# Two-layer MLA / neighbourhood-attention / mixture-of-experts step: where the last tile's down block is loaded, when the next layer's first projection block is loaded, and where a pass issues its row gathers

## What is computed

```python
def grouped_moe(h, w_router, router_bias, w_gate, w_up, w_down):
    scores = sigmoid(t @ w_router)                      # 16 experts in 4 groups
    # best group of 4 experts, then the 2 best experts of it, gates normalised
    act = silu(einsum('td,edf->tef', t, w_gate)) * einsum('td,edf->tef', t, w_up)
    act = act * gates[..., None]
    return einsum('tef,efd->td', act, w_down)           # D = 1024, expert width 256
# per layer
x = x + gate_f * grouped_moe(modulate(rmsnorm(x), shift_f, scale_f))
```

## Time and profile before

| | |
|---|---|
| runs | 1395.22, 1396.58, 1402.12 us |
| profiled execution | 1406.06 us; span of the trace 1404.2 us |
| busy: PE, DVE, ACT, POOL | 1283.3, 568.4, 339.7, 232.8 us |
| chain that ended last | PE 70%, DMA 14%, DVE 6%, issue 5%, ACT 4% |
| of it, the DMA of adds with static lists (`xrows<-big,info`) | 10% |
| of it, the DMA of adds with `last_tok` (`xrows<-big`) | 3% |
| mean granted TensorE clock | 0.978 |
| DMA traffic | 267.82 MB, 191 GB/s over the span |

### The profile page before, as it was taken

The page is one execution under the profiler, slowest core; times in us unless marked ns, Lnnn a source line. Parts: engine busy times, 40 slices in busy tenths (PEclk is TensorE's granted clock), DMA queues, the critical chain, the costliest instruction groups (busy, mean ns, idle before and its releaser), DMA issues.

```text
span 1404.2 us, 19127 instructions
## 1 busy us (share of the span) xinstructions
PE 1283.3 (91%) x7399; PEld 740.6 (53%) x7399; DVE 568.4 (40%) x1454; ACT 339.7 (24%) x823; POOL 232.8 (17%) x298
## 2 busy tenths in 40 slices
PE   5999899999999989998949999999998998999991
PEld 3665466666654554444424455656775446445440
DVE  5122344444535664444322000002664576444443
ACT  3121344444422310000012000003664231000102
POOL 7122300010010012123221100013221001211231
PEclk8999999999999999999979999999999999999996
DMA  9413211122464459999583363145122615999966
GB/s 388 148 39 153 87 62 62 62 105 78 179 247 164 152 193 390 381 380 395 118 249 125 121 225 120 61 173 165 50 66 95 242 62 225 391 379 380 337 171 210
DMA packets 45449, 267.82 MB, mean 191 GB/s; under 512 B 6980, under 2 KB 13460, under 8 KB 31520
## 3 DMA queue, kind: packets, MB, share of 16 engines
q1 hardware_dynamic: 22672, 192.85, 35.1%
q0 software_dynamic: 16928, 52.77, 13.8%
q10 hardware_dynamic: 5760, 20.97, 3.8%
HBM read 230.19 MB, written 34.81 MB: 189 GB/s over the span
## 4 chain that ended last, share of the span: by engine, by line
PE 70%; DMA 14%; DVE 6%; issue 5%; ACT 4%; DVEq 0%; ACTq 0%; POOLq 0%; SPq 0%
PE PS L851 12%; DMA xrows<-big,info 10%; PE PS L1217 10%; PE PS L1079 10%; PE PS L1127 9%; PE PS L723 8%; PE PS L1144 4%; PE PS L979 4%; PE PS L738 3%; DMA xrows<-big 3%; PE PS L1010 2%; PE PS L938 2%; PE PS L1020 2%; DVE big L1621 1%; ACT weights L1481 1%
## 5 line engine op out<-in xcount | busy, mean ns | idle before, releaser
L1079 PE MATMUL PS<-weights,ht 128*128 128x512 f32 x320 | 142.3, 596 | 2.3 <-DVE ht L1621 1.6
L1217 PE MATMUL PS<-ht,weights 128*128 128x128 f32 (+1 forms) x512 | 140.2, 434 | 1.5 <-PE PS L738 0.9
L723 PE MATMUL PS<-const,big 128*128 128x128 f32 (+2 forms) x611 | 90.1, 284 | 37.8 <-DVE big L2151 17.8
L851 PE MATMUL PS<-weights,ht 128*128 128x336 f32 (+1 forms) x320 | 118.2, 528 | 2.6 <-ACT ht L1399 1.6
L1127 PE MATMUL PS<-big 128*128 128x512 f32 x256 | 115.8, 606 | 4.7 <-DVE big L2068 4.7
L723 PEld LDWEIGHTS PS<-const,big 128*128 128x128 f32 (+2 forms) x611 | 74.1, 144 | 84.1 <-issue 58.2
L1217 PEld LDWEIGHTS PS<-ht,weights 128*128 128x128 f32 x512 | 77.8, 191 | 64.1 <-issue 64.1
L1079 PEld LDWEIGHTS PS<-weights,ht 128*128 128x128 f32 x320 | 59.0, 190 | 69.7 <-issue 69.7
L1530 ACT ACTIVATE big<-PS 128x256 f32<-128x256 f32 x34 | 13.1, 385 | 329.4 <-PE PS L1127 329.4
L851 PEld LDWEIGHTS PS<-weights,ht 128*128 128x128 f32 x320 | 61.0, 193 | 54.5 <-issue 41.1
L1127 PE MATMUL PS<-weights,big 128*128 128x512 f32 x192 | 84.4, 592 | 0.0
(11 more groups left out here) (247 smaller groups left out, 1815.3 us busy)
## 6 DMA issues: line engine op xcount, KB each, us to landing
weights<-in_ada SPq DMA_DIRECT2D x22, 2048.0 KB, 8.8
big<-in_gu SPq DMA_DIRECT2D x16, 2048.0 KB, 19.9
weights<-in_gu SPq DMA_DIRECT2D x12, 2048.0 KB, 21.1
rows<-in_down SPq DMA_DIRECT2D x18, 1024.0 KB, 12.4
weights<-in_down SPq DMA_DIRECT2D x16, 1024.0 KB, 16.0
ht<-in_gu SPq DMA_DIRECT2D x6, 2048.0 KB, 22.3
weights<-in_qkv SPq DMA_DIRECT2D x6, 2048.0 KB, 10.2
weights<-in_wo SPq DMA_DIRECT2D x4, 2048.0 KB, 8.6
```

The costliest lines, as they stand in the source:

```text
L723: return pe.transpose(dst, src, const[0:n, C_ID:C_ID + n])
L851: ins = pe.matmul(bank(4 + u % 2, n), lhs(k), rhs(k), start=(k == 0), stop=(k == ks - 1))
L1079: ins = pe.matmul(bank(4 + j), OT[:, k, t * P:(t + 1) * P], w[j][:, k, :], start=(k == 0), stop=(k == KD - 1))
L1217: ins = pe.matmul(bank(bb, n1 - n0), w[:, k, m * P:(m + 1) * P], hT[:, k, n0:n1], start=(k == 0), stop=(k == KD - 1))
```

## The change

In SP's queue the last tile's down block goes to `DN[0]`, behind a wait for the 13th down projection instead of the one that frees `DN[2]`, and in layer 0 the qkv block follows behind a wait for the 14th. POOL's pass issues both gathers in its head: the first before the copies (from list column 5, which is column 3 after the shift), with a wait for its landing before the copies; the second after the copies, before both adds. The two adds then follow one another. PE's last down projection reads `DN[0]`. All engines' instructions are otherwise the same, in number too but for a few waits and one fewer semaphore instruction of POOL's a pass.

```diff
@@ SP @@
-                sp.wait_ge(e_dn[l], trips * 2 + (STAT - 2))
+                sp.wait_ge(e_dn[l], STAT - 2)
                 last = sp.value_load(rtx[0:1, bass.ds(trips * 2 + (STAT - 1), 1)], min_val=0, max_val=E - 1)
-                sp.dma_start(DN[2], a["down"][l][bass.ds(last, 1)]).then_inc(e_dw[l][0], 16)
+                sp.dma_start(DN[0], a["down"][l][bass.ds(last, 1)]).then_inc(e_dw[l][0], 16)
                 if l == 0:
+                    sp.wait_ge(e_dn[l], STAT - 1)
                     static_load(1, 1)
@@ POOL @@
                 with pool.Fori(0, trips) as i:
+                    pool.wait_ge(e_tr[l], i * 2 + (STAT + 1))
+                    pool.nop().then_inc(e_gate, 1)
+                    rows_of(last_token(5), 1)
+                    pool.wait_ge(e_gi[l][1], i * 16 + 16 * 9)
+                    pool.wait_ge(e_gi[l][0], i * 16 + 16 * 8)
                     for par in range(2):
-                        pool.wait_ge(e_gi[l][par], i * 16 + 16 * 8)
                         pool.wait_ge(e_ys[l][par], i * 16 + 16 * 7)
                     pool.nop().then_inc(e_gate, 1)
                     pool.tensor_copy(moved_tok, last_tok[:, 2:15]).then_inc(e_next[l], 1)
...
                     pool.wait_ge(e_next[l], i * 2 + 2)
+                    pool.wait_ge(e_tr[l], i * 2 + (STAT + 2))
                     pool.nop().then_inc(e_gate, 1)
+                    rows_of(last_token(4), 0)
                     for j in range(2):
 
                         pool.wait_ge(e_yd[l], i * 2 + (STAT + j))
                         pool.wait_ge(e_ys[l][1 - j], i * 16 + (112, 128)[j])
                         pool.nop().then_inc(e_gate, 1)
                         add_rows(last_token(j), j)
-
-                        pool.wait_ge(e_tr[l], i * 2 + (STAT + 1 + j))
-                        pool.nop().then_inc(e_gate, 1)
-                        rows_of(last_token(3 + j), 1 - j)
@@ PE @@
-                down(2, e_dw[l][0], trips * 16 + 16, trips * 2 + STAT, None, 3)
+                down(0, e_dw[l][0], trips * 16 + 16, trips * 2 + STAT, None, 3)
```

## The result

The changed kernel takes 1405.23 us (median of 9 runs, 1400.83 to 1408.37), the kernel before 1399.68 us (9 runs, 1395.22 to 1402.25): ratio 1.0028, 95% interval 1.0017 to 1.0039. So it is some 3 us slower. The forecast was 1.0 us faster, and 1405.2 lies outside the range up to 1401.3. Of the 9.6 us between 1395.6 and 1405.2, 3.1 are the reference: the forecast stood on the median of three runs of the kernel before (1396.58), and nine give 1399.68. The other 6.6 are the change's own, 5.6 slower for 1.0 faster by these medians; in the two repeats the medians differ by only 3.0 and 1.9 us. That it stays within 0.5% held.

What follows compares the result with a forecast made beforehand. A handful of adds near each MoE stage's end were taken to set the end. Gains of 0.6 us (first stage) and 0.4 us (second) make 1396.58 - 1.0 = 1395.6 us, range 1391.5 to 1401.3.

Steps and rivals of the forecast that it cites:

- the stretched add 12: First stage: the early qkv block lies over add 12, which takes 10.5 us instead of 7.1 (bounds 7.1 and 11.6).
- Now it lands at 701.11 + 10.91 = 712.02: First stage: add 14's landing before the change, against 712.0 after it; issued 3.8 us later, it gains 3.8 us.
- once getting worse (1404.1): First stage: PE's product of tile 15 runs at the low clock throughout, 3.8 us more; part of a 0.16 chance.
- once gone by the change, as a gain of 3.1 us (1392.5): First stage: PE's wait shifts so that the product at 684 us keeps full clock; chance 0.04.
- 1.9 us of cover remain: Second stage: add 14 lands by 1371.8, add 15 waits for its y until about 1373.7, so the delay costs nothing.
- the prediction's own signs of being wrong: Add 10 or 11 over a microsecond slower, add 12 near 7, second-stage add 15 waiting for add 14, or 5 us off.
- Add 15 without a gather behind it: Both stages: add 15 takes 6.23 us for 6.80 in the first, 6.2 for 6.64 in the second, 0.4 gained there.
- The early down block: First stage: delays add 10 by 0.5 us (bounds nothing and 2.25); second stage: hidden by 2.8 us of cover.
- Clean gain: Rival, chance 0.22: add 12 isn't stretched much, y of tile 15 bounds the first stage's end; 2.5 us faster, 1394.1.
- The slower rival: Chance 0.16: the down block lands on add 10 in full and PE waits; 1400.3 us, or 1404.1 with the clock.
- The row on what 2 MB beside an add cost: Profile row used for add 12's size: 2 MB of qkv beside an add cost it 4.5 us.
- the estimate of an equal share: Add 12: engines alternate between queues, so the block costs it 1.2 us; first stage gains about 1.2 instead of 0.6.

Runs made afterwards that it cites:

- the two repeats: The changed kernel timed twice more with no edit, each beside its own runs of the kernel before: ratio 1.0019 both times.
- the early loads alone: Against the kernel before, only the last down block and the qkv block loaded early, POOL's loop as before: ratio 0.9995.
- the candidate: Against the changed kernel, both gathers of a pass moved behind add 14, loads still early: 0.9992 and 0.9994 to the kernel before.
- the double delay: Two memsets of 2.10 us on POOL ahead of add 14, gathers as before: 1.0023 with early loads, 1.0003 in the kernel before.

## Why the prediction was wrong

**The chain in the changed kernel was forecast well.** From add 12's issue, first stage, in us:

```
                         add 13   g17 landed   add 14   add 15   last add landed
forecast                  11.3       19.2        22.0     29.9      43.1
changed, first trace      11.9       19.6        22.7     29.6      42.6
changed, second trace     12.3         -         23.6     31.2      44.1
changed, third trace      11.4         -         22.3     30.2      43.4
before, first trace        7.8         -         18.7     30.4      44.2
before, second trace       6.9         -         16.5     28.1      41.5
```

The loads, the stretched add 12, the swap of 10.9 against some 6 us for add 14, gather 17's landing (5.8 for 6.0) and the copies came as said. Only gather 18 starts 0.6 us later behind the copies than taken (0.90 us for 0.3), and add 14 took 6.1, 6.8 and 7.1 us in the three traces for the 7.1 taken.

**The step that failed is what it was compared with**: "Now it lands at 701.11 + 10.91 = 712.02", and the 3.56 us for which add 14 was said to wait for its y. Both were read in one execution in which PE's product of tile 15 ran at the low clock. I had this clock before me in two rivals: once getting worse (1404.1), and once gone by the change, as a gain of 3.1 us (1392.5). In both the low clock counted as a property of the kernel before. It was one execution's: in 16 of the 17 traces the product is faster than 9.94 us, and in two of the three of the changed kernel it runs at full clock without any such gain. That it had already made y late, and so padded the cover in front of add 14, I didn't draw. In the second trace of the kernel before, y of tile 15 starts 24.9 us behind add 12's issue (705.48 - 680.58) and not 27.1, the wait in front of add 14 is 2.22 us and not 3.56, and the stage's last add lands 2.6 us sooner. Against that trace the forecast of 43.1 is a loss of 1.6 us, and the three measured stages (mean 43.4) one of 1.9. The reference is one trace; that the early loads alone (41.6 in their trace) timed at 0.9995 speaks for it.

**The second stage** fails in the same way, by a cover read off one execution, but not by the clock: there the product took 7.10 or 7.11 us in every trace. "1.9 us of cover remain" took y of tile 15 at 1372.38, 27.3 us behind add 12's issue. In the second and third trace of the changed kernel it starts 24.6 and 25.0 behind it (1369.51 and 1367.73):

```profile
1369.51 1.28 DVE L1624 TENSOR_TENSOR big<-PS,big 128x512 f32<-128x512 f32 x2
```

In the two traces of the kernel before it is 27.3 and 25.6, in the first of the changed kernel 29.5. How far the chain of adds runs ahead of PE when it reaches add 12 differs by that much from one execution to the next, and the cover with it. In the second and third trace add 14 is issued at 20.2 both times (forecast 19.6), and add 15 follows add 14 by 7.7 us where it follows by 10.5 when y releases it. From y of tile 15 to the read-back of the residual it is 16.9 and 16.7 us instead of 15.5; in the first trace it is 15.6. So the stage costs 1.4, 1.2 and 0.1 us. That add 15 would wait for add 14 there was among the prediction's own signs of being wrong; it came in two traces of three. With the first stage that makes 2.8 us, or 1.002. Between the stages nothing is lost: from the read-back of the first to y of tile 15 in the second it is 645.0, 644.9 and 644.9 us in the changed kernel, 645.6 and 644.9 in the kernel before.

**Sizes that were only off.** Add 15 without a gather behind it gained what was taken in the first stage: add 15 to add 16 is 6.8 to 7.1 us instead of 7.5 and 7.6. In the second it gained nothing: 7.2, 7.5 and 7.7 us instead of 7.4 and 7.3, where a gain of 0.4 us was taken. The early down block cost nothing that shows in the first stage (0.5 taken). In the second it can cost: issued 1.3 to 1.4 us ahead of add 11, in three of the variants with early loads, it left add 11 at 8.5 to 8.7 us; at 1.6 us ahead, in the changed kernel's third trace, at 7.2; at 2.5 us ahead, in its second, at 6.8. The prediction put that behind 2.8 us of cover.

**The rivals.** "Clean gain" needed the end to be bound by y of tile 15. That is reached with the loads alone (0.9995) and with the candidate, but not with the gathers in the head. The slower rival ended on the right side by the wrong mechanism: from add 10 to add 11 it is 10.9, 11.3 and 13.3 us in the three traces, 14.0 and 10.9 in the two of the kernel before. It had no place for the cover in front of adds 14 and 15; that the kernel came out slower at all was luck for it. The row on what 2 MB beside an add cost decided the size of add 12 and was right: 11.1 us, 4.0 more than the 7.1 without the block. The Trainium skill ("DMA: Bandwidth & Descriptors", section "Queues, rings and completion order") lets an engine alternate between queues packet by packet; the estimate of an equal share drawn from it was 2.2 us below what was taken, and this trace doesn't bear it out.

**What stays open.** That the gathers in the head are what costs is shown by leaving them out and by moving them; how much of it is add 14's later start and how much the transfers ahead of it is not separated (see the double delay). The first timing (1.0028) and the repeats (1.0019) agree only by their intervals; the trace sum explains 2.8 of 2.7 to 3.9 us. Whether a share of it lies in how often PE's clock falls wasn't tried: a product slowed by the clock stood in one of three traces of the changed kernel and in one of two of the kernel before. The mean granted clock of an execution is 0.978 to 0.979 over the three timings of the changed kernel and 0.980 over the runs of the kernel before beside the repeats; whether that is cause or effect isn't shown.

## What to carry to other kernels

A cover that is read off one profile is a difference between two chains that both vary: before a wait is called free, read how far the releasing chain was itself late in that execution (here a low granted clock just ahead of it was the sign in the first stage; the second had none), or take a second profile. Work that is issued ahead of the first link of a serial chain is paid as far as nothing else holds that link (3.9 of 4.5 us with early loads, 0.4 of 4.8 with late ones); a place to try for it is behind that link, where the issuing engine waits for the landing anyway. And moving a large transfer off one link of such a chain onto another was worth nothing by itself here: what counts is which of the two links has slack.

## What the runs showed of the hardware that wasn't expected

An accumulating DMA of 128 rows of 4 KB takes some 6 to 7 us with no large load beside it. Beside a 2 MB load it takes 10.7 to 12.6 us with the load issued at about the same time (early loads), 10.8 and 10.9 with it issued 1.5 us ahead, 9.7 to 11.8 with it 2.2 to 2.4 us ahead, 8.0 and 7.8 with it 4.7 and 5.2 us ahead. Where the load was issued at most 1.5 us ahead, the add landed 1.0 to 1.3 us behind the load itself, in the two traces of the kernel before and the first of the changed one. An estimate from the last: the load took 10.0 us, so giving way to as much of its data as the add moves itself, a quarter, would cost 2.5 us; it cost 4.0. So a late start of such a DMA can be nearly free (two memsets, 4.8 us together, cost 0.4 us in the kernel before) or cost nearly in full (3.9 us of 4.5 with early loads), by what else is in flight.

The product of one tile took 7.1, 8.6 to 8.8 or 9.94 us in different executions of nearly the same code. The 9.94 goes with a granted clock of 0.51, the 1.2 GHz level, behind 2.49 us of idling; the three of 8.6 to 8.8 with mean granted clocks of 0.64 to 0.75 over the product's first 5 to 6 us, behind 2.2 to 2.5 us. But 2.57 us of idling in the second trace of the candidate left it at full clock, so the length of the idling alone doesn't say which it will be:

```profile
678.56 7.11 PE L1130 MATMUL PS<-big 128*128 128x512 f32 x16 [2.57 <-DVE big L2071]
```
